# Hybrid attention encoder: pattern C0's scores from stacked split operands, in two fp32r passes

## What is computed

```python
for j, (window, r) in enumerate(((128, 1), (512, 4), (2048, 16))):
    q = rms_norm(per[:, :, j, 0], q_norm)      # 8 heads of 64
    k = rms_norm(per[:, :, j, 1], k_norm)
    v = per[:, :, j, 2]
    o, lse = banded_attention(strided(q), strided(k), strided(v), strided(pos), window // (2 * r), slopes[j])
w = softmax(stack(lses)); o = sum(w * outs)
# banded_attention: s = (q . k) * d**-0.5 - slope * |pos_i - pos_j|, inside the band; softmax; times v
```

## Time and profile before

| what | value |
|---|---|
| median of 3 runs | 2708.42 us (2707.78 to 2709.2) |
| profiled execution, its own time | 2709.8 us |
| its span | 2708.0 us |
| TensorE busy | 2629.4 us, 97% |
| DVE busy | 1639.1 us, 61% |
| ACT busy | 1231.4 us, 45% |
| mean granted TensorE clock | 0.998 |

### The profile page before, as it was taken

One profiled execution on the slowest core, in us unless ns is written; L12 is line 12 of the kernel. 1 busy time (PEld: TensorE's weight loads), 2 busy tenths in 40 slices (PEclk: granted clock), 3 DMA queues, 4 the chain that ended last, 5 costly groups with the idle time before them and its releaser, 6 DMA issues. The chain is left out here.

```text
span 2708.0 us, 36172 instructions
## 1 busy us (share of the span) xinstructions
PE 2629.4 (97%) x12982; PEld 2205.3 (81%) x12982; DVE 1639.1 (61%) x3432; ACT 1231.4 (45%) x2514; POOL 1.5 (0%) x6
## 2 busy tenths in 40 slices
PE   7999999999999999999999999999999999999999
PEld 6999987778877778888779998877788777888887
DVE  6554577545666647676664546775356566485665
ACT  5655545444544334333354555544445443443332
POOL 0000000000000000000000000000000000000000
PEclk9999999999999999999999999999999999999999
DMA  5212223222121332332332122221221213333332
GB/s 184 70 55 79 81 65 92 57 77 72 55 78 48 104 100 88 95 103 88 102 117 71 47 87 74 80 86 55 71 78 56 78 47 109 94 94 101 95 100 94
DMA packets 143874, 225.28 MB, mean 83 GB/s; under 512 B 15046, under 2 KB 69458, under 8 KB 142802
## 3 DMA queue, kind: packets, MB, share of 16 engines
q1 hardware_dynamic: 135842, 201.85, 24.8%
q10 hardware_dynamic: 7856, 21.12, 2.1%
HBM read 210.29 MB, written 12.65 MB: 82 GB/s over the span
## 5 line engine op out<-in xcount | busy, mean ns | idle before, releaser
L1481 DVE TENSOR_TENSOR s_wl<-s_raw,s_wh 128x1024 fp32r<-128x1024 f32 (+2 forms) x376 | 453.2, 1206 | 297.9 <-ACT s_wh L961 297.7
L961 ACT ACTIVATE s_wh<-s_raw 128x1024 fp32r<-128x1024 f32 (+2 forms) x376 | 392.0, 1043 | 396.6 <-PE bank L579 298.3
L579 PE MATMUL bank<-s_hTh,s_wh 128*128 128x512 f32 x1216 | 520.9, 428 | 1.6 <-DVE s_work L1839 1.6
L579 PE MATMUL bank<-s_hTh,s_wl 128*128 128x512 f32 x1216 | 474.7, 390 | 0.0
L579 PE MATMUL bank<-s_hTl,s_wh 128*128 128x512 f32 x1216 | 473.9, 390 | 0.0
L579 PE MATMUL bank<-s_wh,s_hTh 128*128 128x512 f32 (+1 forms) x1088 | 458.1, 421 | 4.5 <-DVE s_early L1621 3.4
L579 PE MATMUL bank<-s_wh,s_hTl 128*128 128x512 f32 (+1 forms) x1088 | 426.2, 392 | 0.0
L579 PE MATMUL bank<-s_wl,s_hTh 128*128 128x512 f32 (+1 forms) x1088 | 425.8, 391 | 0.0
L579 PEld LDWEIGHTS bank<-s_hTh,s_wh 128*128 128x128 f32 x1216 | 228.6, 188 | 69.8 <-issue 23.6
L1278 ACT ACTIVATE s_work<-s_work,s_stat 128x128 f32<-128x128 f32 (+3 forms) x320 | 167.5, 524 | 257.5 <-DVE s_work L2053 113.6
L579 PEld LDWEIGHTS bank<-s_hTl,s_wh 128*128 128x128 f32 x1216 | 228.9, 188 | 66.4 <-issue 24.4
(11 more groups left out here) (202 smaller groups left out, 3408.4 us busy)
## 6 DMA issues: line engine op xcount, KB each, us to landing
s_raw<-in_w_in SPq DMA_DIRECT2D x168, 512.0 KB, 3.6
s_raw<-in_ffn_w_up SPq DMA_DIRECT2D x176, 256.0 KB, 3.1
s_raw<-in_ffn_w_down SPq DMA_DIRECT2D x44, 512.0 KB, 3.7
s_raw<-in_w_branch SPq DMA_DIRECT2D x32, 512.0 KB, 3.7
s_raw<-in_w_o SPq DMA_DIRECT2D x16, 512.0 KB, 3.7
x_keep<-s_work ACTq DMA_DIRECT2D x2, 2048.0 KB, 11.2
s_raw<-in_w_in SPq DMA_DIRECT2D x16, 256.0 KB, 3.0
gate_keep<-s_early ACTq DMA_DIRECT2D x4, 1024.0 KB, 4.3
```

Source lines behind the costliest of these rows:

```text
L579: last = mm(PJ[b][:, 0:width], st, mv, start=i == 0 and n == 1, stop=i == ntiles - 1 and n == 3 * chunks)
L961: a(wh[:, k % 3, 0:n], raw[:, s, 0:n], ACT.Copy).then_inc(*hi_split.up(own))
L1481: v.tensor_tensor(wl[:, k % 3, 0:n], raw[:, k % 2, 0:n], wh[:, k % 3, 0:n].bitcast(F32), ALU.subtract).then_inc(*tile_split.up(own))
```

## The change

C0's keys get the form that A's have, twice, once for the even and once for the odd heads: `kC[half]` holds in its own 64 rows the rounded keys of that half, and in the other 64 rows the rest (key minus rounded key). The first lies where kT was, the second where the second half of `merged` comes later in the layer. C0's queries go to `q_near`, in the place of C2's output and later of the first half of `merged`: part 0 holds the rounded queries in both halves of the rows, part 1 the rest in the own half and zeros in the other. A unit's scores become two fp32r matmuls, part 0 and part 1, added in the bank: rounded queries by rounded keys and by the keys' rest, plus the queries' rest by rounded keys. C0 no longer uses q_pad for its queries, but takes zeros from it.

```diff
 EACH: q_padded=48 -> 32, q_hi=16 -> 32, q_stacked=16 -> 32, q_zeroed=2 -> 4, act_step=189 -> 193, dve_step=534 -> 554
-PADS = dict(C0=16, C1=8, C2=8, B=16)
+PADS = dict(C1=8, C2=8, B=16)
+STACKS = dict(C0=0, A=16, B=32)
...
+    kC = [stacked[:, at:at + 2048].rearrange("p (c n) -> p c n", c=4) for at in (AD + 2048, AD + 12288)]
+    q_near = stacked[:, AD + 10240:AD + 12288].rearrange("p (c h s n) -> p c h s n", c=4, h=2, s=2)
...
 # TensorE, attention(): the waits before a unit's scores
-                        if name == "A":
-                            pe.wait_ge(*q_stacked.at(l, pads_of(name, step)))
+                        if name in STACKS:
+                            pe.wait_ge(*q_stacked.at(l, STACKS[name] + pads_of(name, step)))
...
-                def near_scores(k_of):
-                    def scores_of(u, out):
-                        lo, hi, _mid = near_keys(u)
-                        h = u % 8
-                        return [(out[:, P * lo:P * hi], q_pad[:, h // 2, h % 2, :], k_of(h)[:, P * lo:P * hi], True, True)]
-                    return scores_of
+                def near_scores(u, out):
+                    lo, hi, _mid = near_keys(u)
+                    h = u % 8
+                    return [(out[:, P * lo:P * hi], q_near[:, h // 2, h % 2, part, :],
+                             kC[h % 2][:, h // 2, P * lo:P * hi], part == 0, part == 1) for part in range(2)]
...
-                                     heads_in(9, 12), keys=near_keys)
+                                     heads_in(9, 12) + [q_zeroed.at(l, 2)], keys=near_keys)
...
 # ScalarE, turns(): C0's keys out of the bank
+                    for t in range(4):
+                        yield END["C0k"] + 6.4 + 2 * t
+                        src = group()
+                        for half in range(2):
+                            mine = slice(64 * half, 64 * half + 64)
+                            act.wait_ge(*own.done(l))
+                            a(kC[half][mine, :, P * t:P * t + P], src[mine, :].rearrange("p (c n) -> p c n", c=4), ACT.Copy,
+                              scale=prm[mine, ROW["ckn"]:ROW["ckn"] + 1]).then_inc(*(td_act if half else act_step).up(own))
...
 # ScalarE, pads(): in place of tiles_of("C0", qT, 9, by_pair)
+                def stacks_of_c():
+                    nonlocal done
+                    slot = slots("C0")
+                    done += WINDOW["C0"][2]
+                    for piece in range(8):
+                        t, g = piece // 2, piece % 2
+                        yield slot[4 * piece - 4][1] + 0.8 * slot[0][2] if piece >= 2 else slot[0][1] - 6 + 1.5 * piece
+                        if piece == 0:
+                            act.wait_ge(*td_dve.at(l, 5))
+                            for half in range(2):
+                                other = slice(64 - 64 * half, 128 - 64 * half)
+                                act.wait_ge(*own.done(l))
+                                a(q_near[other, :, half, 1, :], q_pad[other, :, half, :], ACT.Copy).then_inc(*q_zeroed.up(own))
+                        if piece >= 2:
+                            act.wait_ge(*s_ready.at(l, 4 * piece - 4))
+                        for half in range(2):
+                            mine = slice(64 * half, 64 * half + 64)
+                            act.wait_ge(*own.done(l))
+                            a(q_near[mine, 2 * g:2 * g + 2, half, 0, :], qT[mine, 2 * g:2 * g + 2, P * t:P * t + P], ACT.Copy).then_inc(*q_hi.up(own))
...
 # DVE, turns(): C0's keys, in place of k_out
+                    for t in range(4):
+                        yield END["C0k"] + 6.8 + 2 * t
+                        src = group()
+                        for half in range(2):
+                            mine, other = slice(64 * half, 64 * half + 64), slice(64 - 64 * half, 128 - 64 * half)
+                            dve.wait_ge(*own.done(l))
+                            v.scalar_tensor_tensor(kC[half][other, :, P * t:P * t + P], src[mine, :].rearrange("p (c n) -> p c n", c=4), prm[mine, ROW["ckn"]:ROW["ckn"] + 1],
+                                                   kC[half][mine, :, P * t:P * t + P].bitcast(F32), ALU.mult, ALU.subtract).then_inc(*(td_dve if half else dve_step).up(own))
...
 # DVE: a new stream beside stacks()
+            def stacks_c():
+                slot, n = slots("C0"), STACKS["C0"]
+                for piece in range(8):
+                    t, g = piece // 2, piece % 2
+                    yield (slot[4 * piece - 4][1] + 0.8 * slot[0][2] if piece >= 2 else slot[0][1] - 6 + 1.5 * piece) + 0.3
+                    for half in range(2):
+                        n += 1
+                        mine, other = slice(64 * half, 64 * half + 64), slice(64 - 64 * half, 128 - 64 * half)
+                        dve.wait_ge(*q_hi.at(l, n))
+                        dve.wait_ge(*own.done(l))
+                        v.tensor_copy(q_near[other, 2 * g:2 * g + 2, half, 0, :], q_near[mine, 2 * g:2 * g + 2, half, 0, :].bitcast(F32)).then_inc(*dve_step.up(own))
+                        dve.wait_ge(*own.done(l))
+                        v.tensor_tensor(q_near[mine, 2 * g:2 * g + 2, half, 1, :], qT[mine, 2 * g:2 * g + 2, P * t:P * t + P],
+                                        q_near[mine, 2 * g:2 * g + 2, half, 0, :].bitcast(F32), ALU.subtract).then_inc(*q_stacked.up(own))
```

More of the change, by code:

```diff
@@ L123 @@
     pj_dve=108, sq_used=60, normed=53, combined=4, sublayer_normed=4, h_normed=2, h_scaled=2, rstd=3, rows_turned=1, rows_out=1, conv_done=44, td_ready=77, td_act=77, td_dve=77, nt_ready=16, nt_act=24,
-    nt_dve=24, ta_ready=128, ta_act=128, ta_dve=128, q_padded=48, q_hi=16, q_stacked=16, q_zeroed=2, s_ready=144, s_biased=144, p_ready=144, b_mixed=16, o_ready=128, o_out=24,
+    nt_dve=24, ta_ready=128, ta_act=128, ta_dve=128, q_padded=32, q_hi=32, q_stacked=32, q_zeroed=4, s_ready=144, s_biased=144, p_ready=144, b_mixed=16, o_ready=128, o_out=24,
     gains_in=1, ssum=16, lam_dot=1, lam_exp=1, c_diff=2, c_exp=2, merged_sum=24, merged_hi=8, merged_lo=8, conv_mid=44,
-    e_ready=22, hidden_val=22, hidden_hi=22, hidden_lo=22, act_step=189, dve_step=534, params_in=16, direct_in=8,
+    e_ready=22, hidden_val=22, hidden_hi=22, hidden_lo=22, act_step=193, dve_step=554, params_in=16, direct_in=8,
     x_moved=2, c0_moved=6, gates_moved=4,
@@ L899, in heads_in @@
                     return [td_act.at(l, turns_done), td_dve.at(l, turns_done), pj_act.at(l, evacuated)]
-                yield from attention("C0", near_scores(lambda h: kT[:, h // 2, :]),
+                yield from attention("C0", near_scores,
                                      token_values(lambda u, k: vB[:, k, HD * (u % 8):HD * (u % 8) + HD], HD, 8, near_keys), 8,
-                                     heads_in(9, 12), keys=near_keys)
+                                     heads_in(9, 12) + [q_zeroed.at(l, 2)], keys=near_keys)
                 for j in (1, 2):
@@ L910, in attentions @@
                                      token_values(lambda u, k: vA[:, k, HD * (u % 8 // 4):HD * (u % 8 // 4) + HD], HD, 8, near_keys), 8,
-                                     heads_in(57, 72) + [q_zeroed.at(l, 2)], keys=near_keys, tile_of=out_tiles)
+                                     heads_in(57, 72) + [q_zeroed.at(l, 4)], keys=near_keys, tile_of=out_tiles)
                 yield from attention_b(b_scores, heads_in(B_HEADS, 96))
@@ L1213, in turns @@
                         a(lam[:], lam[:], ACT.Exp).then_inc(*lam_exp.up(own))
-                    yield from k_out(END[f"C{j}k"] + 6, CK[j], "ckn")
+                    if j:
+                        yield from k_out(END[f"C{j}k"] + 6, CK[j], "ckn")
+                        continue
+                    for t in range(4):
[6 more added lines that the diff above has]
+                              scale=prm[mine, ROW["ckn"]:ROW["ckn"] + 1]).then_inc(*(td_act if half else act_step).up(own))
                 for t in range(4):
@@ L1339, in residues_of @@
                         a(q_pad[part, :, h % 2, :], CQ[j][part, h // 2, :].rearrange("p (r n) -> p r n", r=RES), ACT.Copy).then_inc(*q_padded.up(own))
-                by_pair, by_map = (lambda g: slice(2 * g, 2 * g + 2)), (lambda g: slice(g, 4, 2))
-                yield from tiles_of("C0", qT, 9, by_pair)
+                by_map = lambda g: slice(g, 4, 2)
+                yield from stacks_of_c()
                 for j in (1, 2):
@@ L1942, in turns @@
                     lo_out(gTl[:, 0:4, cols], gTh[:, 0:4, cols], group(), td_dve, gain[:, 20:21])
+            def stacks_c():
[12 more added lines that the diff above has]
+                                        q_near[mine, 2 * g:2 * g + 2, half, 0, :].bitcast(F32), ALU.subtract).then_inc(*q_stacked.up(own))
             def stacks():
-                slot, n = slots("A"), 0
+                slot, n = slots("A"), STACKS["A"]
                 for piece in range(8):
@@ L2084, in attentions @@
                 yield from attention_b()
```

(2 more changed lines are left out.)

## The result

The changed kernel takes 2717.64 us (median of 10 runs, 2713.26 to 2720.25) beside 2708.57 us before (10 runs, 2706.25 to 2712.77): a ratio of 1.0031, with a 95% interval of 1.0022 to 1.0041. The prediction was 2700.4 us with a range of 2693 to 2707.5; the change makes the kernel slower by 0.3%, 17.2 us from the forecast and outside the range. The profiled execution took 2713.67 us with a span of 2711.9 us. In `after` the dense matmuls are on line 584, turns on 619, values on 808, scores on 820, DVE's copy of the probabilities on 2038, its bias on 2102, its copy of the output bank on 2116, its queries out of the turns' bank on 1907 and its key operation on 1940; ACT's key operation is on 1227.

A forecast was written before the change was run, and what follows sets the result against it. TensorE was taken as the bound, busy 2629.4 of 2708.0 us. Terms -17.0 + 4.1 + 4.9 = -8.0 us took the profiled 2709.8 to 2701.8; the median, 1.4 lower, was forecast at 2700.4 us, range 2693 to 2707.5.

The forecast's parts named there:

- the passes: C0's score matmuls on TensorE: two fp32r passes save 0.31 or 0.22 us a unit, -17.0 us in all.
- keys and start: Key turns and first units of C0: waits for ACT's and DVE's longer key operations, 2.2 + 0.8 + 1.1 = 4.1 us.
- the pieces: DVE's stacked-query work in C0, eight groups a layer of two casts and two subtractions: 2.45 us a layer, 4.9 in both.
- The matmuls: Step on C0's scores: took the saving between starts from A's rows, 17.0 us over 32 units of each width.
- lower bound: Least saving of C0's score matmuls, taken from busy times: 14.0 us.
- pieces 4 and 7: Fifth and eighth groups of DVE's stacked-query work: TensorE waits 0.75 and 1.2 us in layer 1.
- piece 3: Fourth group of DVE's stacked-query work, near 122 us: delays emptying the output bank at a tile's end, 0.4 us.
- piece 5: Sixth group of DVE's stacked-query work, near 149 us: DVE idles about 1 us, copy and bias fit, cost 0.
- The clock: Granted clock in C0: single waits lose none in the sum; a pair of waits in A lost 1.7 us more.
- slower rival: DVE's stacked-query work in C0 causes paired waits and lower clock, 3.4 us each: +11, 2719 us; chance 0.05.
- the passes get no shorter: C0's score matmuls save nothing while the added work costs 4.1 + 4.9 = +9: 2717 us; chance 0.03.
- The hidden case: DVE's stacked-query work fits its idle time in C0, only key turns show: 2691.4 to 2694 us, about 2693; chance 0.21.

The follow-up runs named there:

- passes_alone: Changed kernel with the keys leaving the bank as before and DVE's stack operations left out, low parts of C0's scores missing; 2700.97 us.
- no_pieces: Changed kernel without DVE's 32 stack operations a layer, so the queries' low part is missing, new keys kept; 2705.82 us.
- pieces_late: Changed kernel with DVE's stack operations split into halves, from the third group on placed behind DVE's copy and bias, one unit apart; 2715.82 us.
- best2: Changed kernel with overlapped key halves on ACT and DVE, layer 1's A bias tables moved after C0, and stack halves behind the output copy; 2705.97 us.

## Why the prediction was wrong

| term | predicted | medians | what the profile shows |
|---|---|---|---|
| the passes | -17.0 | -8.2 | units' stretch -8.9 |
| keys and start | +4.1 | +4.85 alone | key stretch +4.7, unit 1's wait 0.9 |
| the pieces | +4.9 | +8.1 alone | units' stretch +8.1 |
| keys and pieces together | +9.0 | +16.7 | both stretches +14.3 |
| sum | -8.0 | +8.5 | |

The sum of the medians is +8.5 by subtraction alone, passes_alone being in it twice; it differs from the +9.1 between before and after only by the two medians of before. In the profiles both stretches grow by 5.6 us from before to after (255.2 to 260.8), less than the medians; after's profiled execution, 2713.67, is the second fastest of its ten.

- **The step that failed is in "The matmuls":** "I take 17.0, since starts are the firmer reading; the row of A has the same weight load, the same width and the same neighbours." The unit's own weight load and width are the same; the neighbours are not. Behind C0's scores stand dense matmuls with 310 ns loads, behind A's with 188. That the record of a score matmul is as short as in A was right (19.4 and 15.0 us), and so even the "lower bound" of 14.0 was none: here busy time saved was not start saved, for the next matmul waited for its load. This is 8.8 of the 17.2 us; keys and pieces together are 7.7, and 0.7 is the drift of before's median and rounding. Of the 8.8, the loads' share by the unit distances is 15.4 - 10.6 = 4.8; 17.0 - 15.4 = 1.6 is in the 256-key unit, which even with short loads saves 0.19 and not 0.22, and the 384-key one, with 0.29 and not 0.31; of the remaining 2.4, laid-bare waits are 1.1, and the rest is open.
- **The pieces** were the right mechanism, mis-sized: 2.45 us a layer forecast, 8.1/2 = 4.05 measured. The waits at pieces 4 and 7 are there, with none at 2 and 6, but piece 3's is double (it delays the output bank and also the probabilities), and a turn at 159.42 us, 5 us behind piece 5, waits 0.36 for the queries, where I had 0 for piece 5. I had laid the pieces on before's timeline; that the shorter units leave DVE less room is my reading, and no run tests it alone.
- **The keys** were near: 3.84 us between turns (82.92, 86.76) and not 3.56, for ACT's two operations take 1.40 and not 1.3, DVE's 1.53 and not 1.47, and the hand-overs between them 0.9 and not 0.8. The rows that I named, 689 and 751 ns, give 1.38 and 1.50 for two; I had taken less than they say. The last turn of layer 1 waits 1.45 (91.57), as forecast.
- **The clock.** In the profile it stayed as forecast: the granted clock over C0's units is 1.00 after, as in the earlier trace rows, in spite of six waits of 0.36 to 1.37 us. By the Trainium skill (TensorE: Matmul & The Clock Gate, A second HAM failure mode: psum-queue depth-cycling) small idle times between groups of (bf16) matmuls, if frequent enough, make the clock go down and up; this execution doesn't show that. But keys and pieces together take 14.3 us in the profile's stretches and 16.7 in the medians. The mean granted clock over the runs is 0.9964 after and 0.9977 in no_pieces, and 0.0013 of 2705 is 3.5 us. Of the runs with a clock of 0.997, after's are at 2715.5 (3 runs) and no_pieces' at 2706.4 (3 runs), 9.1 apart. So some 3 of the 11.8 us between the two medians go with a lower clock in some executions; that is an estimate, since the clock of a run is on record in steps of 0.001, or 2.7 us. Whether the waits bring that about is open: pieces_late, with as many waits, has 0.9971.
- **The rivals.** The time is near that of the slower rival (2719) and of "the passes get no shorter" (2717), and by neither's way: no pair of waits of 3.4 us, and passes that did get shorter, by half. The hidden case was also added up wrongly: -17 + 1 to 3 is 2692.4 to 2694.4 us, and not 2691.4 to 2694.

## What to carry to other kernels

Before a saving is taken over from another stage, compare the instructions around it in both, their weight loads above all: here the shorter matmuls paid only until they laid bare the next load. Work added to a busy engine's fixed queue costs by what stands right behind it, so move it by fractions of a slot and read the new list of waits, since the first move may only shift them. When a change has a gain and two preparations, run the gain alone first: here it had 8 us, and the preparations as placed cost 13 to 17; best2, with the same parts placed otherwise, is 0.12% faster than before (0.9980 to 0.9997).

## What the runs showed of the hardware

- In the dense blocks a stationary operand of 128x128 four-byte elements read with a stride of four elements loads in 310 to 318 ns, one read side by side in 188. The Trainium skill (TensorE: Matmul & The Clock Gate, LDWEIGHTS) lets the time of a load go by its columns, by its formula 107 ns for 128; here 128 columns take 188 or 310, and the measurement decides.
- GpSimd's subtraction of 64x256 takes 865 ns where DVE's takes 419, and while it runs, DVE's operations of 128x32 with two inputs in the same memory take up to 0.77 us instead of 0.19 (in C0 on average 0.33). Copies out of a bank kept their 0.29. The Trainium skill (GPSIMD Engine Reference, Key points) says that GpSimd shares its memory interfaces with DVE, in contention with DVE's operations with two inputs there; the trace agrees.
- The granted clock differs between executions of one program, from 0.995 to 0.998 after, and the time goes with it: 2720.2 us at 0.995, 2713.3 at 0.998.
